# x and the first weight unit in four pieces each, on two DMA queues

## The reference

```python
def _rmsnorm(x, g):
    xf = x.astype(jnp.float32)
    y = xf * lax.rsqrt(jnp.mean(xf * xf, axis=-1, keepdims=True) + EPS)
    return (y * g.astype(jnp.float32)).astype(x.dtype)
...
        h = _rmsnorm(x, norm_g[layer])
        if layer % 2 == 0:
            i = layer // 2
            proj = jnp.einsum('bsd,de->bse', h, e_w_in[i])
            u_val, u_gate, z_a, q_b, k_b, v_b, z_b = _split(proj, EVEN_SIZES)
            y_a = _conformer_conv(u_val, u_gate, a_conv_w[i], a_conv_b[i], a_ln_g[i], a_ln_b[i]) * jax.nn.silu(z_a)
            q = _rmsnorm(_split_heads(q_b, N_HEADS), b_qnorm_g[i])
            k = _rmsnorm(_split_heads(k_b, N_HEADS), b_knorm_g[i])
            v = _split_heads(v_b, N_HEADS)
            y_b = _merge_heads(_moba_attention(q, k, v, slopes)) * jax.nn.silu(z_b)
            y = jnp.concatenate([y_a, y_b], axis=-1)
        ...
        x = x + jnp.einsum('bse,ed->bsd', y, w_out[layer]).astype(x.dtype)
    return x
```

## Time and profile before

| | |
|---|---|
| median of the timed runs | 920.67 us (920.03 to 921.87) |
| profiled execution, its own time | 918.58 us |
| its span, first to last instruction | 916.8 us |
| PE busy | 888.8 us (97%) |
| POOL, ACT, DVE busy | 620.4, 444.1, 429.2 us |
| mean granted TensorE clock | 0.994 |
| HBM read | 174.95 MB |

### The profile page before, as it was taken

How to read it: one execution, slowest core, us unless ns; L and a number is a source line. 1 busy time by engine, 2 the same in 40 slices (tenths; PEclk the granted TensorE clock), 3 DMA queues, 4 the chain that set the end, 5 groups by cost and what they waited for, 6 DMA issues and landing times.

```text
span 916.8 us, 16544 instructions
## 1 busy us (share of the span) xinstructions
PE 888.8 (97%) x6840; PEld 828.4 (90%) x6840; DVE 429.2 (47%) x901; ACT 444.1 (48%) x654; POOL 620.4 (68%) x485
## 2 busy tenths in 40 slices
PE   6999999999998999999999999999999999989997
PEld 5898888998777999878988899999999999989996
DVE  3998665203875476873464223231134674531001
ACT  3434664444656453344345447676426675523330
POOL 0766466850000669889776777768889899999880
PEclk9999999999999999999999999999999999999999
DMA  9844548861420279587666435445536555535421
GB/s 346 339 152 162 206 170 329 297 233 39 167 93 1 92 296 395 215 348 274 229 229 206 164 139 178 144 143 185 192 137 266 192 187 188 193 115 184 184 92 46
DMA packets 27906, 177.60 MB, mean 194 GB/s; under 512 B 3080, under 2 KB 5780, under 8 KB 7480
## 3 DMA queue, kind: packets, MB, share of 16 engines
q1 hardware_dynamic: 26248, 174.35, 52.3%
q10 hardware_dynamic: 1584, 2.20, 0.7%
HBM read 174.95 MB, written 3.43 MB: 195 GB/s over the span
## 4 chain that ended last, share of the span: by engine, by line
PE 78%; POOL 9%; DVE 5%; ACT 3%; DMA 2%; issue 2%; ACTq 0%; DVEq 0%; SPq 0%
PE proj L727 15%; PE proj L729 15%; PE proj L730 15%; POOL w_lo L641 7%; PE proj L702 5%; PE proj L763 3%; PE proj L1003 3%; PE proj L810 2%; PE proj L811 2%; PE proj L808 2%; DMA raw<-in_weights 2%; POOL w_lo_b L641 1%; POOL w_lo_a L641 1%; PE mixed L955 1%; PE proj L1078 1%
## 5 line engine op out<-in xcount | busy, mean ns | idle before, releaser
L641 POOL TENSOR_TENSOR w_lo<-raw,w_hi 128x512 fp32r<-128x512 f32 (+2 forms) x336 | 429.3, 1313 | 217.7 <-ACT w_hi L1367 217.7
L729 PE MATMUL proj<-parts,w_lo 128*128 128x256 f32 x952 | 266.3, 280 | 0.6 <-POOL w_lo L641 0.6
L727 PE MATMUL proj<-parts,w_hi 128*128 128x256 f32 x904 | 257.2, 285 | 0.2 <-ACT arena L1392 0.2
L730 PE MATMUL proj<-parts,w_hi 128*128 128x256 f32 x904 | 252.5, 279 | 0.0
L1367 ACT ACTIVATE w_hi<-raw 128x2048 fp32r<-128x2048 f32 (+2 forms) x84 | 158.9, 1894 | 115.3 <-DMA raw<-in_weights 62.1
L729 PEld LDWEIGHTS proj<-parts,w_lo 128*128 128x128 f32 x952 | 179.1, 188 | 1.6 <-POOL w_lo L641 0.8
L727 PEld LDWEIGHTS proj<-parts,w_hi 128*128 128x128 f32 x904 | 169.9, 188 | 2.3 <-issue 1.6
L730 PEld LDWEIGHTS proj<-parts,w_hi 128*128 128x128 f32 x904 | 170.3, 188 | 0.0
L641 POOL TENSOR_TENSOR w_lo<-arena,w_hi 128x512 fp32r<-128x512 f32 x36 | 48.8, 1391 | 43.2 <-ACT w_hi L1367 43.1
L727 PE MATMUL proj<-hid_hi,w_hi 128*128 128x256 f32 x160 | 46.2, 288 | 3.5 <-POOL w_lo L641 3.5
L729 PE MATMUL proj<-hid_hi,w_lo 128*128 128x256 f32 x160 | 45.7, 285 | 0.0
(11 more groups left out here) (385 smaller groups left out, 2111.8 us busy)
## 6 DMA issues: line engine op xcount, KB each, us to landing
raw<-in_weights SPq DMA_DIRECT2D x104, 1024.0 KB, 5.1
arena<-in_weights SPq DMA_DIRECT2D x35, 1024.0 KB, 6.3
wide<-in_weights SPq DMA_DIRECT2D x9, 1024.0 KB, 6.8
probT<-in_weights SPq DMA_DIRECT2D x8, 1024.0 KB, 5.2
dil_lines<-dil_line SPq DMA_DIRECT2D x1, 2304.0 KB, 14.2
raw<-in_weights SPq DMA_DIRECT2D x3, 512.0 KB, 6.1
dil_bias<-dil_lines SPq DMA_DIRECT2D x1, 1536.0 KB, 9.9
xT<-in_x SPq DMA_DIRECT2D x2, 512.0 KB, 5.8
```

Of the source, the lines that this page charges most:

```text
L641: nc.gpsimd.tensor_tensor(lo_slots[RAW_AT[n]][:, at], raw_slots[RAW_AT[n]][:, at], hi_slots[HI_AT[m]][:, at].bitcast(F32), ALU.subtract).t ...
L727: nc.tensor.matmul(dst, whi, h, start=first, stop=False)
L729: nc.tensor.matmul(dst, wlo, h, start=False, stop=False)
L730: last = nc.tensor.matmul(dst, whi, lo[:, k, :], start=False, stop=stop)
```

## The change

x comes in four DMAs of two tiles (256 KB) each, all issued by SyncE, one directly behind the other. The first unit comes in four DMAs of two tiles (256 KB) each, issued by ScalarE, between its narrow DMA and the one with the other vectors. Each piece has a semaphore of its own, and each reader waits for the piece that it reads. SyncE's other DMAs, the matmuls and their order stay as they are.

```diff
-        x_in = [sem("x_in0"), sem("x_in1")]
+        x_in = [sem(f"x_in{i}") for i in range(4)]
+        first_unit_in = [sem(f"uv0_in{i}") for i in range(3)] + [raw_in[RAW_AT[0]]]
...
-            for i, half_in in enumerate((sem("uv0_half"), raw_in[RAW_AT[0]])):
-                at = slice(UNIT // 2 * i, UNIT // 2 * (i + 1))
-                sp.dma_start(xT[:, 4 * i:4 * i + 4], cut(a["x"], S)[:, 4 * i:4 * i + 4]).then_inc(x_in[i], 16)
-                sp.dma_start(raw_slots[RAW_AT[0]][:, at], a["weights"][0][:, at]).then_inc(half_in, 16)
+            for i in range(4):
+                sp.dma_start(xT[:, 2 * i:2 * i + 2], cut(a["x"], S)[:, 2 * i:2 * i + 2]).then_inc(x_in[i], 16)
...
-                pe.wait_ge(sem("uv0_half"), 16)
                 for k in range(KD):
                     pe.wait_ge(sem("x_scaled"), k + 1)
-                    if k == KD // 2:
-                        pe.wait_ge(raw_in[RAW_AT[0]], raw_target(0))
+                    if k % 2 == 0:
+                        pe.wait_ge(first_unit_in[k // 2], 16)
...
             act.dma_start(cols[:, 0:16], a["vectors"][:, 0:16]).then_inc(sem("norm_g_in"), 16)
+            for i in range(4):
+                at = slice(UNIT // 4 * i, UNIT // 4 * (i + 1))
+                act.dma_start(raw_slots[RAW_AT[0]][:, at], a["weights"][0][:, at]).then_inc(first_unit_in[i], 16)
             act.dma_start(cols[:, 16:], a["vectors"][:, 16:]).then_inc(first_in, 16)
             act.wait_ge(first_in, 16)
             table(ACT.Sqrt)
             for i in range(4):
-                stream_squares(2 * i, 2 * i + 2, (x_in[i // 2], 16))
+                stream_squares(2 * i, 2 * i + 2, (x_in[i], 16))
...
-                dve.wait_ge(x_in[k // 4], 16)
+                dve.wait_ge(x_in[k // 2], 16)
```

## The result

| | before | changed |
|---|---|---|
| median of the timed runs | 920.03 us (917.11 to 921.87, 5 runs) | 926.78 us (925.33 to 929.6, 5 runs) |
| ratio | | 1.009, 95% interval 1.0061 to 1.012 |
| profiled execution, its own time | 918.58 us | 926.71 us |
| span | 916.8 us | 924.9 us |
| PE busy | 888.8 us | 891.2 us |

The change makes the kernel slower: by 6.75 us between the medians, by 8.13 us between the two profiled executions. The ratio takes in all ten runs (their means give 1.0087, the medians 1.0073); its interval is 5.6 to 11.0 us. The forecast was 926.0 us, with 921.5 to 929.0 as the range.

The account below looks back on a forecast made before the run. TensorE was taken as the bound, busy 888.8 of 916.8 us, with the start passed on in full. 3.4 us for later sums plus 1.9 for the clock gave +5.3 on 920.67: 926.0 us, range 921.5 to 929.0.

Parts of the forecast that it names:

- The early start and its worth: First unit: TensorE starts at about 6.1 us, 1.2 us sooner, ends at 15.5, then stands 4.4 us, so worth nothing.
- The late `first_in`: Vectors' DMA, last on ScalarE's queue: lands at 14.9 instead of 7.6 us; sums start 3.4 us later.
- the late bound of 16.7: Latest expected landing of first_in, 16.7 us, from how long small took; total then +7.4 us, 928.1 us.
- The path from `first_in` to the sums: ScalarE's squares and VectorE's folds take 4.87 us, plus 0.1 for semaphores; sums start at 19.9 us.
- The clock: After TensorE's 4.4 us stand the granted clock falls, also on ug0; costs 1.9 us, bounds 1.64 and 2.2.
- The rival in which the clock stays up: Second rival, at the sums and ug0: sums late but clock stays up; +3.4 us, 924.1 us; 14%.
- A share by bytes: At ScalarE's queue: sharing by bytes lands first_in by about 10.6 us, so nothing stands; 919.5 us; 10%.
- the third rival: At the queues: SyncE sends two DMAs per ScalarE DMA; first_in near 19.9 us, +10.3 us, 931.0 us; 4%.
- any shift of the start: Behind the start everything hangs on TensorE's results, so a shift of the start passes to the end in full.
- the rival with the gain: First rival, at the start: first_in lands by about 10.6 us, only the earlier start remains; 1.2 us less, 919.5; 10%.
- The fourth rival: Behind the start: TensorE's shorter later waits take up delay, only 1.3 us in the first 115 us; 924.5 us; 5%.
- the equal counts that were to show the mechanism: Sign at the DMA queues: equal packet counts on both queues between 9 and 12 us.

Follow-up runs that it names:

- run with small packets: Changed kernel with ug0 and uv1 on SyncE's queue each loaded in four 256 KB DMAs (2 KB a partition instead of 8 KB); 923.81 us, ratio 1.005.
- the run with the vectors ahead: Changed kernel with both DMAs of vectors ahead of the four unit pieces on ScalarE's queue; 925.05 us, ratio 1.0047.
- the split alone: Kernel before, x and unit still in halves, but the unit's halves issued by ScalarE ahead of its second DMA of vectors; 927.22 us, ratio 1.0073.
- the pieces alone: Changed kernel with quarter pieces of x and unit by turns, all on SyncE's queue; ScalarE issues the vectors as before; 919.44 us, ratio 0.9996.
- the run with the filled stand: Changed kernel with 15 more fp32 matmuls behind the first unit, filling TensorE's wait before the sums; 924.19 us, ratio 1.0053.
- vectors between the pieces: Changed kernel with all x and unit pieces on SyncE's queue and the second vectors DMA there behind the second pair; 918.31 us, ratio 0.9998.

## Why the prediction was right

**The early start and its worth.** Forecast: TensorE starts at 6.1 us, ends the unit at 15.5 us, and the lead is lost in the stand. Measured 5.69 and 15.97 us; the lead was larger, and the unit took 10.28 us instead of 9.32: 0.53 of the 0.96 us more are a wait for its last piece, which landed at 13.8 rather than 11.7 us. That the lead is worth nothing held.

**The late `first_in`.** The mechanism held: the pairs of one DMA on either queue, the vectors last. The run with small packets shows the turns, the run with the vectors ahead shows that it is the place in the queue, and the runs with the split alone and with the pieces alone show that the split makes the loss. The size was off: 14.9 us forecast, 17.9 us measured, beyond even the late bound of 16.7, and 18.9, 19.1 and 20.2 us in other executions with the same DMAs. This is the term of the sum that was mis-sized, by 3 us. Two parts of it can be read in the changed kernel. One is the slow stretch; its windows, of which the kernel before has no like:

```profile
5.00:6.00 1.00, 0.31 (x1) 1.00 1.03 330
6.00:7.00 1.00, 1.00 (x3) 1.00 0.69 150
7.00:8.00 1.00, 1.00 (x4) 1.00 0.89 309
```

At 0.42 MB a microsecond 1.26 MB would have gone in these three, and 0.79 did: 1.1 us, of which a faster 4 to 5 us gives some back. The 4.49 MB of the forecast's last pair had gone by 14.7 us, where the sum has 13.9 (the landing at 14.9 less the 1 us that it holds between data and landing): 0.8 us.

The other is the end of ScalarE's queue. Each DMA sends 128 rows and 16 packets of 4 bytes, which fit the 16 by which its semaphore rises; six DMAs are 864 packets on this queue, and x, `ug0` and `uv1` are 864 on SyncE's. The pairs of the forecast have both through at the same time. The packets of the changed kernel from 0 to 15 us, then from 0 to 17 us:

```profile
q1 hardware_dynamic: 879, 3.30, 57.1%
q10 hardware_dynamic: 834, 1.30, 26.0%
q1 hardware_dynamic: 983, 4.07, 62.0%
q10 hardware_dynamic: 864, 1.34, 23.6%
```

SyncE's queue was 38 packets ahead already at 5 us, since it could start on x while ScalarE's had only the narrow DMA, and was still 36 ahead at 14 us. And the last packets of ScalarE's queue came one by one (9 from 15.5 to 16 us, 4 behind that), the last at 16.6 us. That is 1.9 us behind the 864th of SyncE's. From there to the landing it took 1.3 us, 0.3 more than the 1 us in the sum. Together 0.8 + 1.9 + 0.3 = 3.0 us.

This tail is also what differs between the executions. SyncE's 864th packet went at 14.6 to 14.8 us in the four profiles with these DMAs, ScalarE's at 16.6, 18.1, 18.1 and 19.6 us, and `first_in` came at 17.9, 18.9, 19.1 and 20.2 us. In the latest one only five packets went behind 17 us. Why a few packets of a queue lag is not shown.

**The path from `first_in` to the sums.** Forecast 4.87 us and 0.1 for the semaphores; measured 22.92 - 17.91 = 5.01.

**The clock.** Forecast: low, at 1.9 us, between 1.64 and 2.2. Measured 2.3 us by the run with the filled stand, a little over the bound: `ug0`'s first half lost 1.85 us, as in the rows, and the sums took 0.98 instead of 0.58 us, which the term had left out. The rival in which the clock stays up did not happen in the changed kernel's two profiles; in the run with small packets it did, once of twice.

**The other rivals.** A share by bytes is refuted by the packet counts. So is the third rival, two of SyncE's DMAs for each of ScalarE's, with `first_in` near 19.9 us. The second profile, at 20.2 us, would fit it by the time alone; but up to 15 us SyncE's queue had sent 877 packets in it and ScalarE's 823, far from two to one, and it is the last packets that were late. The Trainium skill's page "DMA: Bandwidth & Descriptors" (Queues, rings and completion order) says that an engine drains a packet of some 9 to 17 descriptors from one ring before it switches. The traces do not bear this out for these loads, if a row is a descriptor. Equal counts would fit turns of any equal length, but they are even in short stretches too: in the eleven half microseconds from 9.5 to 15 us ScalarE's queue sent 19 to 28 packets in each. With turns of nine rows, in which an engine sends none of them for over 2 us (nine rows of 8 KB at about 0.3 us) and then nine in about 0.7 us, I estimate far larger swings. As far as these runs show, the queues change over after one row or two.

Nothing behind the start took the delay up, as said: +8.75 us at the spread, +8.37 us at 186 us. But the prediction's "any shift of the start" goes on to the end in full holds for a delay only. Of a lead of 1.58 and of 1.84 us (one queue; vectors between the pieces) 0.25 us were left at 186 us. In the rival with the gain, 1.2 us would have been too much.

**Slips, and a sign.** `small` is issued 0.24 us behind `first_in` (18.15 us) and not behind the squares, 2.5 us later as the forecast had it; nothing hangs on it. The fourth rival's time should read 924.7 (926.0 - 1.3), not 924.5. From 9 to 12 us the two queues sent 49, 41 and 51 against 45, 45 and 49 packets, the equal counts that were to show the mechanism.

**The total.** 5.3 us were forecast on the sum of two terms, 3.4 and 1.9. The start of the profiled execution lost 6.4 and 2.3, 8.7 us. That the time came out at 926.78 against 926.0 us owes something to chance: the medians differ by 6.75 us, the profiled pair by 8.13, in which the low clock at 216 us takes 1.7 back (both profiles of the kernel before had it, neither of the changed kernel; I have not shown why) and the last stretch adds 0.9 again. By the ratio the loss is 8.3 us, and the forecast 5.3 lies under its interval of 5.6 to 11.0. The base helped too: 920.67 us was the median of three runs of before, that of the five is 920.03. So the direction and the two terms are understood, but the closeness of the time is partly luck.

## What to carry to other kernels

Two DMA queues on the same engines take turns by packets, so a small DMA that stands behind others on the less loaded queue is not served by its own size: it pays, for every row ahead of it and of its own, one row of the other queue's large DMAs. Before a queue is filled with early pieces, list what stands behind them on it and who waits for that, since here a 279 KB load of constants became the head of the path. And a stand of TensorE costs more than its length, if the clock falls in it, here 2.3 us for 7 us of waiting. A delay at the start of the path goes on to the end, but a lead lasts only until the first wait for another engine: look for the side chains that it will meet before counting it.

## What the runs showed that I had not expected

The clock does not follow the length of the stand alone. It fell to 0.50 after a stand of 1.81 us (the halves on two queues) and after 3.29 us, and stayed at 1.00 after 2.85 us in the same program, and through two waits of 1.20 and 1.37 us. In all executions that had one of 2.3 to 3.4 us near 850 us, a low clock followed.

The packets that raise the semaphores take turns too, at nine to eight in each DMA and engine. They do so on both queues, so that one DMA still goes with one DMA.

Quarter pieces on both queues, the unit directly behind the narrow DMA, brought a microsecond of 150 GB/s at 6 to 7 us in every execution that had them (150 to 193 GB/s in seven profiles), whether TensorE stood or not; with the vectors' DMA between the narrow one and the unit it was not there. The two queues aren't needed for a dip: with all quarter pieces on SyncE's queue it was 227 GB/s at 7 to 8 us, or 200 GB/s from 6 to 8 us with the vectors between them.

An execution differs from the next by where the clock is low and by the tail of a queue, not by the work: the same stretch of 184.3 us took 187.8 to 189.3 us when TensorE happened to wait at 850 us. A gain of 1.6 to 1.8 us at the start isn't seen in the time, and most of it is gone from the trace as well by 186 us.
